# Two first weight loads as plain float32, the input in two transfers, and the angles' sines later, in a fused two-block transformer kernel

## The chip, the cores and the metric

The kernel runs on one core of one Trainium2 chip. The metric is the device time of one execution in microseconds (us). Three runs of the kernel before gave 1520.52, 1523.52 and 1526.42 us, so the median is 1523.52 us. The profile is of one more execution, which took 1524.71 us; the span that its trace covers is 1522.6 us.

## The reference

A sequence of 256 positions with 1024 features passes through two transformer blocks. The change touches the opening of the first block and one side computation for the second. Cut to that:

```python
# first block
h = rms_norm(x, norm_mix_g)                 # x is 256 x 1024
proj = h @ w_in                             # 1024 x 7168: b, c, x, a, g, gate_sc, gate_cf
cf = (cf_a + bias_a) * sigmoid(cf_g + bias_g)
y_cf = causal_depthwise_conv(cf, cf_conv_w)         # 31 taps
y_sc = sc_b * causal_depthwise_conv(sc_c * sc_x, sc_conv_w)   # 3 taps
# ... output projections, memory attention, an expert layer with gathered rows
# second block: attention with rotary positions, sines and cosines of
# positions * frequency, and with a bias by distance, then an MLP
```

Everything is float32.

## The kernel before

Features lie on the 128 partitions, the 256 positions along the free axis, so a projection of two output tiles (256 output features) is: two PSUM banks, each summed over eight 128x128 weight pieces `k`. One weight load is 1 MB (128 x 2048 words) and holds the pieces of two such tiles. The loads are numbered in the order of the list `LOADS`: 0 is for tiles g0 and g1, 1 for a0 and a1, 2 for g2 and g3, 3 for a2 and a3, and so on up to 7 (a6, a7); then follow, block by block, `c`, `x`, `b`: load 8 is c0 and c1, load 9 is x0 and x1, load 10 is b0 and b1, load 11 is c2 and c3, load 12 is x2 and x3, load 13 is b2 and b3.

Precision is kept by splitting. ScalarE copies a load from `raw` into a rounded part `w_hi` (line 1086), then VectorE or GpSimd takes the rest, `w_lo = raw - w_hi` (line 508). Activations are split in the same way into `x_hi` (line 1063, ScalarE) and `x_lo` (line 1438, VectorE). TensorE makes three matmuls of each pair (lines 678 to 680: hi by hi, hi by lo, lo by hi). `raw`, `w_hi` and `w_lo` are rings of three slots each (`RING = 3`). `LO_BY` says by name which engine subtracts: GpSimd has load 2 and 5, and every load from 8 to 19; VectorE has 0, 1, 3, 4, 6 and 7.

Each engine has its own instruction stream, written out by hand, and the order within it is the order of the code; engines wait on semaphores.

- SyncE issues the transfers: `x`, the small vectors, loads 0 and 1, constants, the memory input, positions, subkeys, and then the loads from 2 on. Load `i` waits until the `w_lo` of load `i - 3` is made (its slot of `raw` is then free).
- ScalarE: `round_to(n)` makes `w_hi` up to load n; `drain(name, i)` calls `ahead(name, i)` first (`round_to` up to two loads beyond this tile's load) and then copies the tile out of PSUM. The rounding of load `i` also waits until the last tile of load `i - 3` is finished, since it overwrites its halves. ScalarE squares `x` for the norm, makes load 0's `w_hi`, takes the square root (line 1105), splits the normed tiles, drains g0 to g7, then waits for `rope_arg` (line 1179), takes two `Sin` activations (lines 1180 and 1181), and only then goes on with c0.
- VectorE: waits for the vectors, makes load 0's `w_lo`, takes the reciprocal (line 1419), and alternates norm tiles (line 1454) with `x_lo` tiles. In the loop over the a tiles it drains each one (line 1512), and between a6 and a7 it runs `rope_angles` (lines 1484 to 1504), a chain in which every instruction waits for the one before it (`link`) and which reads and writes SBUF alone. Then come convolution taps (line 1540, sums in PSUM) between the drains of x and b tiles.
- TensorE: the sums of squares (line 728), then the tiles in the order of the list. There are four accumulation banks; a tile waits until the tile four before it has been drained. Thus x1 waits for a7's drain, and x2 for b0's.

The change and the steps of the prediction touch `linear_wide` (line 695), `linear` (682), the ScalarE stream from line 1161 to 1190, the VectorE stream from 1477 to 1522, `load` (526) and `wait_halves_free` (497).

Of the kernel before, what the change touches and what calls it, by code (L numbers as in the profile page):

```python
# [24 lines left out]
P = 128  # L25
SEQ = 256
# [141 lines left out]
for _, _, _e in TILES:  # L168
# [6 lines left out]
            )  # L175
BY_DVE = range(LOAD_OF["pq", 12], LOAD_OF["up", 6])
WHOLE = range(BEFORE_GATHERS + 1, LOAD_OF["gb", 7] + 1)
SLOTS = 11
# [16 lines left out]
for _i in range(len(LOADS)):  # L195
    HI_COUNT.append(_i + 1 - sum(_j <= _i for _j in WHOLE))
    RAW_COUNT.append(sum(_j % RING == _i % RING and _j not in WHOLE for _j in range(_i + 1)))
    if _i in WHOLE:
        LO_BY.append(None)
        continue  # L200
    _e = "pool" if _i % 3 == 2 and _i not in BY_DVE or LOADS[_i] in DVE_BUSY else "dve"
    _seen[_e] += 1
    LO_BY.append((_e, _seen[_e]))
# [46 lines left out]
def two_blocks(nc, T):  # L250
    ctx = ExitStack()
    with ctx:
# [165 lines left out]
        subkeys_landed = sem("subkeys_landed")  # L418
        x_landed = sem("x_landed")
        mem_landed = sem("mem_landed")  # L420
# [76 lines left out]
        def wait_halves_free(eng, i):  # L497

            if i >= RING and i - RING not in WHOLE:
                eng.wait_ge(acc_ready, LAST_TILE[i - RING] + 1)  # L500
            elif i - RING in WHOLE:
                eng.wait_ge(acc_ready, max(LAST_TILE[OCCUPANT[at]] for at in slots_of(i)[1:]) + 1)
# [19 lines left out]
        def _(sp):  # L522
            sp.dma_start(x_res[:].rearrange("p (t s) -> p t s", t=DT),
                         T["x_t"].rearrange("(t p) s -> p t s", p=P)).then_inc(x_landed, 16)

            def load(i):
                name, b = LOADS[i]
                if i >= RING and i - RING not in WHOLE:
                    engine, n = LO_BY[i - RING]
                    sp.wait_ge(w_lo_ready[engine], n)  # L530
                elif i - RING in WHOLE:
                    sp.wait_ge(acc_ready, LAST_TILE[OCCUPANT[i % RING]] + 1)
                sp.dma_start(ring(raw, i), T[name][b]).then_inc(raw_landed[i % RING], 16)
# [35 lines left out]
        def _(pool):  # L569
# [13 lines left out]
            def subtract_to(last):  # L583
                while n_lo[0] <= min(last, len(LOADS) - 1):
                    if n_lo[0] not in WHOLE and LO_BY[n_lo[0]][0] == "pool":
                        w_lo_split(pool, g, n_lo[0])
                    n_lo[0] += 1
# [44 lines left out]
        def _(pe):  # L632
# [24 lines left out]
            def linear_whole(name, which, wname, b, cols, lo=0, rows=P):  # L657

                w = whole_slot(wname, b)
                for j, i in enumerate(which):  # L660
                    out = open_tile(name, i)
                    for k in range(DT):
                        at = k * cols + lo + j * P
                        pe.wait_ge(h_ready, DT + k + 1)
                        mm = nc.tensor.matmul(by_chunk(out[0:rows, 0:SEQ]), w[:, at:at + rows], h_tile(k),  # L665
                                              start=(k == 0), stop=(k == DT - 1))
                    mm.then_inc(acc_ready, 1)

            def halves(x, k, cols=slice(0, SEQ)):
# [149 lines left out]
            for b in range(4):  # L819
                if b == 0:  # L820
                    linear_wide("g", range(2), "w_in", 16, "h1")
                else:
                    linear("g", range(2 * b, 2 * b + 2), "w_in", 16 + b, "h1", DT, 256)
                linear("a", range(2 * b, 2 * b + 2), "w_in", 12 + b, "h1", DT, 256)
                if b == 1:
# [217 lines left out]
        def _(act):  # L1043
# [34 lines left out]
            def round_to(last):  # L1078
                while n_hi[0] <= min(last, len(LOADS) - 1):
                    i = n_hi[0]  # L1080
                    n_hi[0] += 1
                    if i in WHOLE:
                        continue
# [76 lines left out]

            act.wait_ge(x_landed, 16)
            square("mix", lambda k: None, x_res)
            act.wait_ge(filled, 8)
            round_to(0)
            root("mix")
            split_all("h1", normed_tile("mix"), h_norm)
            round_to(1)
            for b in range(4):
# [8 lines left out]
                elif b == 2:  # L1177
                    split_all("mem", normed_tile("mem"), mem_raw)
            act.wait_ge(rope_arg, 2)
            s.activation(sin_t[NOPE:QHB, :], sin_t[NOPE:QHB, :], ACT.Sin).then_inc(rope_ready, 1)  # L1180
            s.activation(cos_t[NOPE:QHB, :], cos_t[NOPE:QHB, :], ACT.Sin).then_inc(rope_ready, 1)
            for b in range(4):
                for i in range(2 * b, 2 * b + 2):
                    drain("c", i, ct(c_buf, i))
                ahead("x", 2 * b)
                ahead("b", 2 * b)
            for i in range(8):
                drain("gsc", i, ct(gate_sc, i), ACT.Sigmoid)
# [221 lines left out]
        def _(dve):  # L1410
# [57 lines left out]
            def subtract_to(last):  # L1468
                while n_lo[0] <= min(last, len(LOADS) - 1):
                    if n_lo[0] not in WHOLE and LO_BY[n_lo[0]][0] == "dve":  # L1470
                        w_lo_split(dve, w_, n_lo[0])
# [4 lines left out]

            dve.wait_ge(vec_landed, 16)
            subtract_to(0)
            norm_split("mix", x_res, "norm_mix_g", h_norm, "h1")
            subtract_to(1)  # L1480

# [613 lines left out]
```

## Time and profile before

| | |
|---|---|
| median of three runs | 1523.52 us |
| the profiled execution | 1524.71 us |
| its span | 1522.6 us |
| TensorE (PE) busy | 1341.1 us, 88% |
| VectorE (DVE) busy | 957.4 us, 63% |
| ScalarE (ACT) busy | 523.3 us, 34% |
| GpSimd (POOL) busy | 559.6 us, 37% |

In the rows below, PE is TensorE, PEld its weight load, DVE is VectorE, ACT is ScalarE, POOL is GpSimd and SP is SyncE. Times are in us from the start of the span, "ns" apart. A row of the timeline is: start, duration, engine, line, operation, what it writes and reads with their shapes, the number of instructions merged, and in brackets how long the engine sat idle before it and what released it. A matmul's duration reaches to its modelled end; matmuls overlap, so the distance from one start to the next is the rate. PEclk is the share of full speed that TensorE's clock was granted (1.00 is 2.4 GHz, 0.50 is 1.2 GHz).

### The profile page before, as it was taken

To read this page: it belongs to the slowest core of one execution; us is meant where nothing else is said; L and a number is where in the kernel's file an instruction comes from. 1 tells how busy PE (TensorE), PEld (TensorE's weight loads), DVE (VectorE), ACT (ScalarE), POOL (GpSimd) and SP (SyncE) were. 2 spreads that over 40 slices of the span, in tenths; PEclk is the share of its full clock that TensorE was granted. 3 is DMA by queue.
4 is the path that set the end of the run, shared out by engine and by line. 5 is a ranking of instruction groups with operands and counts; after the bars stand their busy time and mean duration, and the time that the engine had idled before them with its cause. 6 is when DMAs were issued, how large, how long until landed. Compare 5 with 4: busy or idle time off the path is not lost.

```text
span 1522.6 us, 26124 instructions
## 1 busy us (share of the span) xinstructions
PE 1341.1 (88%) x10156; PEld 1280.4 (84%) x10156; DVE 957.4 (63%) x2043; ACT 523.3 (34%) x993; POOL 559.6 (37%) x348
## 2 busy tenths in 40 slices
PE   6999999899897868787878887978899999899996
PEld 6989999798897868786878877878785789899996
DVE  4698955765379585857676677755424447673563
ACT  6444454455443212121212221211226455444341
POOL 1377851321364546454535453545002000022230
PEclk9999999899999999898999998999999999999998
DMA  7445553352359999999999999999930134245450
GB/s 279 162 156 176 194 173 134 138 173 95 121 197 421 421 422 421 422 422 422 422 421 420 420 420 422 421 422 422 393 141 1 32 135 167 86 164 199 164 192 28
DMA packets 58071, 397.40 MB, mean 261 GB/s; under 512 B 6272, under 2 KB 9856, under 8 KB 10368
## 3 DMA queue, kind: packets, MB, share of 16 engines
q0 software_dynamic: 36864, 268.45, 42.5%
q1 hardware_dynamic: 21120, 127.76, 23.7%
q8 instruction: 58, 0.95, 0.3%
q14 instruction: 29, 0.24, 0.0%
HBM read 395.14 MB, written 1.05 MB: 260 GB/s over the span
## 4 chain that ended last, share of the span: by engine, by line
PE 49%; DMA 22%; DVE 15%; issue 8%; ACT 3%; POOL 2%; DVEq 0%; POOLq 0%; SPq 0%; ACTq 0%
DMA rows_late<-peer_uv_dram,stage 21%; PE bank L678 11%; PE bank L679 10%; PE bank L680 10%; PE bank L665 6%; PE bank L891 5%; DVE rows_late L1827 4%; PE bank L728 2%; ACT w_hi L1086 1%; POOL w_lo L508 1%; PE bank L789 1%; DMA rows_late<-peer_uv_dram,expert 1%; DVE w_lo L508 1%; POOL rows_late L608 1%; DVE probs L1775 1%
## 5 line engine op out<-in xcount | busy, mean ns | idle before, releaser
L508 POOL TENSOR_TENSOR w_lo<-raw,w_hi 128x2048 fp32r<-128x2048 f32 x49 | 227.5, 4645 | 517.5 <-ACT w_hi L1086 517.5
L891 PE MATMUL bank<-h_norm,rows_late 128*128 128x128 f32 x2816 | 331.7, 281 | 31.5 <-ACT h_norm L1254 31.5
L891 PEld LDWEIGHTS bank<-h_norm,rows_late 128*128 128x128 f32 x2816 | 327.5, 197 | 34.8 <-ACT h_norm L1254 34.8
L1827 DVE SCALAR_TENSOR_TENSOR rows_late<-rows_late,squares 128x1024 f32<-128x1024 f32 x176 | 213.7, 1228 | 135.0 <-DMA rows_late<-peer_uv_dram,stage 130.8
L891 PE MATMUL bank<-h_norm,rows_early 128*128 128x128 f32 x1280 | 176.2, 305 | 92.2 <-ACT h_norm L1254 92.1
L891 PEld LDWEIGHTS bank<-h_norm,rows_early 128*128 128x128 f32 x1280 | 170.0, 218 | 98.9 <-ACT h_norm L1254 98.9
L608 POOL DMA_INDIRECT rows_late<-peer_uv_dram,stage x165 | 197.0, 1194 | 136.1 <-PE bank L891 79.9
L508 DVE TENSOR_TENSOR w_lo<-raw,w_hi 128x2048 fp32r<-128x2048 f32 x55 | 133.5, 2429 | 129.0 <-ACT w_hi L1086 123.0
L678 PE MATMUL bank<-x_hi_a,w_hi 128*128 128x256 f32 x704 | 204.6, 291 | 10.9 <-DVE x_lo_a L1438 6.0
L1086 ACT ACTIVATE w_hi<-raw 128x2048 fp32r<-128x2048 f32 x104 | 197.7, 1904 | 47.5 <-PE bank L680 47.0
L678 PE MATMUL bank<-x_hi_b,w_hi 128*128 128x256 f32 x640 | 189.0, 295 | 20.6 <-POOL w_lo L508 10.7
L679 PE MATMUL bank<-x_lo_a,w_hi 128*128 128x256 f32 x704 | 200.6, 285 | 0.0
L680 PE MATMUL bank<-x_hi_a,w_lo 128*128 128x256 f32 x704 | 200.5, 285 | 0.0
L679 PE MATMUL bank<-x_lo_b,w_hi 128*128 128x256 f32 x640 | 185.5, 290 | 0.0
L680 PE MATMUL bank<-x_hi_b,w_lo 128*128 128x256 f32 x640 | 185.2, 289 | 0.0
L1254 ACT ACTIVATE h_norm<-const,weight 128x128 f32<-128x128 f32 x256 | 82.0, 390 | 291.5 <-DVE weight L1821 279.1
L608 POOL DMA_INDIRECT rows_early<-peer_uv_dram,stage x75 | 89.6, 1195 | 169.2 <-PE bank L891 145.8
L678 PEld LDWEIGHTS bank<-x_hi_a,w_hi 128*128 128x128 f32 x704 | 136.4, 194 | 13.2 <-issue 6.4
L678 PEld LDWEIGHTS bank<-x_hi_b,w_hi 128*128 128x128 f32 x640 | 127.5, 199 | 23.0 <-POOL w_lo L508 11.5
L1827 DVE SCALAR_TENSOR_TENSOR rows_early<-rows_early,squares 128x1024 f32<-128x1024 f32 x80 | 97.1, 1225 | 65.7 <-DMA rows_early<-peer_uv_dram,stage 53.7
L679 PEld LDWEIGHTS bank<-x_lo_a,w_hi 128*128 128x128 f32 x704 | 136.5, 194 | 0.5
L680 PEld LDWEIGHTS bank<-x_hi_a,w_lo 128*128 128x128 f32 x704 | 136.5, 194 | 0.0
(297 smaller groups left out, 2007.5 us busy)
## 6 DMA issues: line engine op xcount, KB each, us to landing
raw<-w_in_dram SPq DMA_DIRECT2D x28, 1024.0 KB, 4.9
raw<-w_up_dram SPq DMA_DIRECT2D x16, 1024.0 KB, 4.9
raw<-w_down_dram SPq DMA_DIRECT2D x16, 1024.0 KB, 4.9
rows_late<-w_in_dram SPq DMA_DIRECT2D x10, 1024.0 KB, 13.6
raw<-w_kv_dram SPq DMA_DIRECT2D x8, 1024.0 KB, 4.9
raw<-w_peer_q_dram SPq DMA_DIRECT2D x8, 1024.0 KB, 4.8
raw<-sc_w_out_dram SPq DMA_DIRECT2D x4, 1024.0 KB, 4.8
raw<-cf_w_pw_dram SPq DMA_DIRECT2D x4, 1024.0 KB, 4.9
```

Source lines behind the costliest of these rows:

```text
L508: api.tensor_tensor(ring(w_lo, i), ring(raw, i), ring(w_hi, i).bitcast(F32), ALU.subtract).then_inc(w_lo_ready[LO_BY[i][0]], 1)
L608: g.indirect_dma_start(out=expert_rows(k), out_offset=None, in_=T["peer_uv"], in_offset=bass.IndirectOffsetOnAxis(ap=stage_at[:, k:k + 1], ...
L665: mm = nc.tensor.matmul(by_chunk(out[0:rows, 0:SEQ]), w[:, at:at + rows], h_tile(k), start=(k == 0), stop=(k == DT - 1))
L678: nc.tensor.matmul(out, s_hi, m_hi, start=first, stop=False)
L679: nc.tensor.matmul(out, s_hi, m_lo, start=False, stop=False)
L680: return nc.tensor.matmul(out, s_lo, m_hi, start=False, stop=last)
L728: mm = nc.tensor.matmul(STAT[:, 0:SEQ], ones[:], ct(src, k), start=(k == 0), stop=(k == kt - 1))
L789: mm = nc.tensor.matmul(SCORE[u % 2][:, SEEN_BY[c]], q[:, c * P:(c + 1) * P], k[:, 0:(c + 1) * P], start=True, stop=True)
L891: mm = nc.tensor.matmul(ct(Y_ACC[c][t // 4], t % 4, P), expert_rows(k)[:, D + t * P:D + (t + 1) * P], ct(diag, k % DIAGS, P), start=False, ...
L1086: s.activation(ring(w_hi, i), ring(raw, i), ACT.Copy).then_inc(w_hi_ready, 1)
L1254: s.activation(ct(diag, k % DIAGS, P), ident, ACT.Copy, scale=weight[:, side * TOPK + k:side * TOPK + k + 1]).then_inc(diag_ready, 1)
L1827: w_.scalar_tensor_tensor(out=row, in0=row, scalar=1.0, in1=h_tok[:, c * D:(c + 1) * D], op0=ALU.mult, op1=ALU.mult, accum_out=pre[:, side ...
```

## The change

Loads 0 and 1 are not split. TensorE multiplies them as plain float32 from `raw`, as soon as each normed tile is there, in a new function `linear_plain`; their slots of `raw` are free only when their last tile is finished, so loads 3 and 4 wait for that. ScalarE's two roundings and VectorE's two subtractions for them go. VectorE makes all eight norm tiles first and the `x_lo` tiles after them. The input `x` comes in two transfers of four feature tiles each, and the squares of the second half wait for the second. The two `Sin` activations stand after the drains of the c tiles and the roundings up to load 21, twelve loads later.

```diff
+PLAIN = range(2)
-    HI_COUNT.append(_i + 1 - sum(_j <= _i for _j in WHOLE))
+    HI_COUNT.append(_i + 1 - sum(_j <= _i for _j in (*PLAIN, *WHOLE)))
...
-            sp.dma_start(x_res[:].rearrange("p (t s) -> p t s", t=DT),
-                         T["x_t"].rearrange("(t p) s -> p t s", p=P)).then_inc(x_landed, 16)
+            for half in range(2):
+                tiles = slice(half * DT // 2, (half + 1) * DT // 2)
+                sp.dma_start(x_res[:].rearrange("p (t s) -> p t s", t=DT)[:, tiles],
+                             T["x_t"].rearrange("(t p) s -> p t s", p=P)[:, tiles]).then_inc(x_landed[half], 16)
...
-                if i >= RING and i - RING not in WHOLE:
+                if i - RING in PLAIN:
+                    sp.wait_ge(acc_ready, LAST_TILE[i - RING] + 1)
+                elif i >= RING and i - RING not in WHOLE:
...
+            def linear_plain(name, which, i):
+                pe.wait_ge(raw_landed[i % RING], 16 * RAW_COUNT[i])
+                outs = [open_tile(name, n) for n in which]
+                for k in range(DT):
+                    pe.wait_ge(normed, NORMED["mix"] - DT + k + 1)
+                    for j, out in enumerate(outs):
+                        at = k * 256 + j * P
+                        mm = nc.tensor.matmul(out[:, 0:SEQ], ring(raw, i)[:, at:at + P], ct(h_norm, k),
+                                              start=(k == 0), stop=(k == DT - 1))
+                        if k == DT - 1:
+                            mm.then_inc(acc_ready, 1)
...
                 if b == 0:
-                    linear_wide("g", range(2), "w_in", 16, "h1")
+                    linear_plain("g", range(2), LOAD_OF["g", 0])
+                    linear_plain("a", range(2), LOAD_OF["a", 0])
                 else:
                     linear("g", range(2 * b, 2 * b + 2), "w_in", 16 + b, "h1", DT, 256)
-                linear("a", range(2 * b, 2 * b + 2), "w_in", 12 + b, "h1", DT, 256)
+                    linear("a", range(2 * b, 2 * b + 2), "w_in", 12 + b, "h1", DT, 256)
...
-            act.wait_ge(x_landed, 16)
-            square("mix", lambda k: None, x_res)
+            square("mix", lambda k: act.wait_ge(x_landed[k // 4], 16), x_res)
             act.wait_ge(filled, 8)
-            round_to(0)
             root("mix")
             split_all("h1", normed_tile("mix"), h_norm)
-            round_to(1)
...
-            act.wait_ge(rope_arg, 2)
-            s.activation(sin_t[NOPE:QHB, :], sin_t[NOPE:QHB, :], ACT.Sin).then_inc(rope_ready, 1)
-            s.activation(cos_t[NOPE:QHB, :], cos_t[NOPE:QHB, :], ACT.Sin).then_inc(rope_ready, 1)
             for b in range(4):
                 for i in range(2 * b, 2 * b + 2):
                     drain("c", i, ct(c_buf, i))
                 ahead("x", 2 * b)
                 ahead("b", 2 * b)
+            act.wait_ge(rope_arg, 2)
+            s.activation(sin_t[NOPE:QHB, :], sin_t[NOPE:QHB, :], ACT.Sin).then_inc(rope_ready, 1)
+            s.activation(cos_t[NOPE:QHB, :], cos_t[NOPE:QHB, :], ACT.Sin).then_inc(rope_ready, 1)
...
-            subtract_to(0)
-            norm_split("mix", x_res, "norm_mix_g", h_norm, "h1")
-            subtract_to(1)
+            norm("mix", x_res, "norm_mix_g", h_norm)
+            split_all("h1", h_norm)
```

## Rows read from the trace of the kernel before

**Rows 1.** The page's part 4: the chain that ended last, by engine.
```profile
PE 49%; DMA 22%; DVE 15%; issue 8%; ACT 3%; POOL 2%; DVEq 0%; POOLq 0%; SPq 0%; ACTq 0%
```

**Rows 2.** Stretch: start:end, length, PE busy (instructions), PEclk, DMA share, GB/s.
```profile
90.00:240.00 150.00, 150.00 (x1240) 1.00 0.55 190
```

**Rows 3.** The opening, timelines of ACT, DVE and PE.
```profile
6.48 2.56 ACT L1055 ACTIVATE squares<-x_res 128x256 f32<-128x256 f32 x8 [4.47 <-DMA x_res<-x_t_dram]
12.78 0.47 ACT L1105 ACTIVATE root_buf<-bank,eps 128x256 f32<-128x256 f32 x1
...
11.57 2.29 DVE L508 TENSOR_TENSOR w_lo<-raw,w_hi 128x2048 fp32r<-128x2048 f32 x1 [11.57 <-ACT w_hi L1086]
13.78 1.75 DVE L1419 RECIPROCAL rstd<-root_buf 128x256 f32<-128x256 f32 x1
...
7.04 5.71 PE L728 MATMUL bank<-squares,mean_d 128*128 128x256 f32 x16 [7.04 <-ACT squares L1055]
17.10 0.36 PE L678 MATMUL bank<-x_hi_a,w_hi 128*128 128x256 f32 x1 [4.36 <-DVE x_lo_a L1438]
25.65 0.39 PE L678 MATMUL bank<-x_hi_a,w_hi 128*128 128x256 f32 x1 [1.06 <-DVE w_lo L508]
```

**Rows 4.** A stretch of the first transfers: all engines, PEclk, DMA share, GB/s.
```profile
4.50:5.00 0.50, 0.00 (x0) 0.00 (x0) 0.00 (x0) 0.00 (x0) 0.00 (x0) 1.00 1.07 383
```

**Rows 5.** First and last of tile x1's 24 matmuls, from PE's timeline.
```profile
78.37 0.39 PE L678 MATMUL bank<-x_hi_a,w_hi 128*128 128x256 f32 x1
...
81.23 0.28 PE L680 MATMUL bank<-x_hi_a,w_lo 128*128 128x256 f32 x1
```

**Rows 6.** From the chain in order of time: eight plain float32 matmuls.
```profile
43.19 3.45 PE bank L728 x16
```

**Rows 7.** Around the angles and b0: timelines of ACT, DVE, POOL and PE.
```profile
78.57 1.92 ACT L1086 ACTIVATE w_hi<-raw 128x2048 fp32r<-128x2048 f32 x1
...
66.83 0.48 DVE L1512 SCALAR_TENSOR_TENSOR cf_in<-bank,vec,sig 128x256 f32<-128x256 f32 x1 [5.48 <-PE bank L680]
67.23 3.85 DVE L1484 CAST pos_row<-probs 128x256 f32<-128x256 int32 x1
...
71.91 0.29 DVE L1491 TENSOR_TENSOR dist<-dist,turns 128x128 f32<-128x128 f32 x1
...
73.41 0.34 DVE L1493 TENSOR_SCALAR sin_t<-pos_row,const 32x256 f32<-32x256 f32 x1
...
77.83 0.48 DVE L1512 SCALAR_TENSOR_TENSOR cf_in<-bank,vec,sig 128x256 f32<-128x256 f32 x1
...
93.48 0.42 DVE L1570 TENSOR_TENSOR c_buf<-bank,c_buf 128x256 f32<-128x256 f32 x1
...
66.31 4.62 POOL L508 TENSOR_TENSOR w_lo<-raw,w_hi 128x2048 fp32r<-128x2048 f32 x1 [0.46 <-ACT w_hi L1086]
80.57 13.69 POOL L508 TENSOR_TENSOR w_lo<-raw,w_hi 128x2048 fp32r<-128x2048 f32 x3 [9.64 <-ACT w_hi L1086]
...
85.19 0.39 PE L678 MATMUL bank<-x_hi_a,w_hi 128*128 128x256 f32 x1 [3.68 <-POOL w_lo L508]
```

**Rows 8.** Other meetings of DVE and POOL, from their timelines.
```profile
58.59 2.76 DVE L1438 TENSOR_TENSOR x_lo_b<-cf_acc,x_hi_b 128x256 fp32r<-128x256 f32 x8
60.25 5.59 POOL L508 TENSOR_TENSOR w_lo<-raw,w_hi 128x2048 fp32r<-128x2048 f32 x1 [15.82 <-ACT w_hi L1086]
...
428.67 4.61 POOL L508 TENSOR_TENSOR w_lo<-raw,w_hi 128x2048 fp32r<-128x2048 f32 x1 [0.71 <-ACT w_hi L1086]
...
432.69 0.62 DVE L1771 TENSOR_SCALAR part_i<-fin_i 128x32 uint32<-128x32 uint32 x1
```

**Rows 9.** PE's clock behind a pause; stretches as in Rows 2.
```profile
18.00:19.00 1.00, 1.00 (x7) 0.50 1.00 418
89.00:90.00 1.00, 1.00 (x8) 0.68 0.26 107
287.00:289.00 2.00, 2.00 (x17) 0.85 0.59 246
```

More of the change, by code:

```diff
@@ L195 @@
 for _i in range(len(LOADS)):
-    HI_COUNT.append(_i + 1 - sum(_j <= _i for _j in WHOLE))
+    HI_COUNT.append(_i + 1 - sum(_j <= _i for _j in (*PLAIN, *WHOLE)))
     RAW_COUNT.append(sum(_j % RING == _i % RING and _j not in WHOLE for _j in range(_i + 1)))
-    if _i in WHOLE:
+    if _i in WHOLE or _i in PLAIN:
         LO_BY.append(None)
@@ L418, in two_blocks @@
         subkeys_landed = sem("subkeys_landed")
-        x_landed = sem("x_landed")
+        x_landed = [sem(f"x_landed{i}") for i in range(2)]
         mem_landed = sem("mem_landed")
@@ L497, in wait_halves_free @@
         def wait_halves_free(eng, i):
-            if i >= RING and i - RING not in WHOLE:
+            if i >= RING and i - RING not in WHOLE and i - RING not in PLAIN:
                 eng.wait_ge(acc_ready, LAST_TILE[i - RING] + 1)
@@ L522, in _ @@
         def _(sp):
-            sp.dma_start(x_res[:].rearrange("p (t s) -> p t s", t=DT),
-                         T["x_t"].rearrange("(t p) s -> p t s", p=P)).then_inc(x_landed, 16)
+            for half in range(2):
+                tiles = slice(half * DT // 2, (half + 1) * DT // 2)
+                sp.dma_start(x_res[:].rearrange("p (t s) -> p t s", t=DT)[:, tiles],
+                             T["x_t"].rearrange("(t p) s -> p t s", p=P)[:, tiles]).then_inc(x_landed[half], 16)
             def load(i):
                 name, b = LOADS[i]
-                if i >= RING and i - RING not in WHOLE:
+                if i - RING in PLAIN:
+                    sp.wait_ge(acc_ready, LAST_TILE[i - RING] + 1)
+                elif i >= RING and i - RING not in WHOLE:
                     engine, n = LO_BY[i - RING]
@@ L584, in subtract_to @@
                 while n_lo[0] <= min(last, len(LOADS) - 1):
-                    if n_lo[0] not in WHOLE and LO_BY[n_lo[0]][0] == "pool":
+                    if n_lo[0] not in WHOLE and n_lo[0] not in PLAIN and LO_BY[n_lo[0]][0] == "pool":
                         w_lo_split(pool, g, n_lo[0])
@@ L1081, in round_to @@
                     n_hi[0] += 1
-                    if i in WHOLE:
+                    if i in WHOLE or i in PLAIN:
                         continue
@@ L1469, in subtract_to @@
                 while n_lo[0] <= min(last, len(LOADS) - 1):
-                    if n_lo[0] not in WHOLE and LO_BY[n_lo[0]][0] == "dve":
+                    if n_lo[0] not in WHOLE and n_lo[0] not in PLAIN and LO_BY[n_lo[0]][0] == "dve":
                         w_lo_split(dve, w_, n_lo[0])
```

## The prediction

> **What bounds the kernel now.** I read the page's chain first. It gives PE 49% and DMA 22% [rows 1]. The DMA part belongs to the expert rows, far behind the change, so all that the change can do is to let everything behind the opening start earlier or later. I then read the timelines of PE for its pauses in the first 240 us. There are few: before 7.04, before 17.10, before 25.65 and before 85.19 [rows 3, 7]; from 90 to 240 it is busy for all of 150.00 us [rows 2]. So PE is the bound of this stage, VectorE has pauses in it, and a shift of PE at 90 us should arrive at the end whole. The change works on all four pauses. What is to be seen: the first is a DMA wait, the second is the norm's chain, the third is the split of load 1, and the last is b0 waiting for GpSimd's `w_lo` of load 10, which is late because ScalarE rounded it only at 78.57, after the two sines [rows 7].
>
> **The opening.** Before, x1's 24 matmuls start 0.12 us apart (78.37 to 81.23), so a piece of a tile costs 0.36 us and a tile 2.88 [rows 5]. A plain float32 matmul of the same width is two instructions, eight of them take 3.45 us, 0.43 each [rows 6]. The 32 pieces of g0, g1, a0, a1 thus cost 32 x 0.43 = 13.8 us of PE instead of 32 x 0.36 = 11.5: the edit adds 2.3 us of matmul. What it takes away is the chain ahead of it.
>
> Input in halves: ScalarE squares from 6.48 [rows 3]. Half of x is 0.52 MB, and at 383 GB/s [rows 4] that is 1.37 us, so the first half should land at about 5.1 and the second as before. ScalarE's eight squares take 2.56 us, but PE takes 5.71 for their sums [rows 3], against 3.45 for the same work later [rows 6]: it works at about half speed at first, so PE, not ScalarE, ends this step (7.04 + 5.71 = 12.75, the root follows at 12.78). Starting at 5.7 instead of 7.04 they end at 11.4, if the full clock comes as soon after the start; if it comes at the same moment as before, the lost lead is worth up to half of 1.3, so 12.1. I take 11.6. The extra issue on SyncE is hidden: nothing waits for its queue before the loads, and they are bound by bytes.
>
> From root to product: root to reciprocal was 12.78 to 13.78, because VectorE subtracted load 0 until 11.57 + 2.29 = 13.86; without it the reciprocal can start half a microsecond behind the root. Root 11.6, reciprocal at 12.15 for 1.75, first norm tile at 13.9, ready at 14.4. PE starts at 14.45 (before 17.10, since x_hi and x_lo stood between). PE's pace (0.86 for the two pieces of one k) is slower than VectorE's, so nothing starves it. After a similar pause PE ran at clock 0.50 at 18 to 19 us, and around 89 it was still coming back [rows 9]; behind the pause before 85.19 this lasted 3.4 us, a loss of 1.7 us. I charge 1.7 here too: a1 ends at 14.45 + 13.8 + 1.7 = 29.95. Before it ended at 25.65 + 16 x 0.36 = 31.4 (rounded up by the slower first matmul: 31.45). Gain 1.5 us. Bounds: a gain of 3.2 if the shorter pause (2.8 us instead of 4.4) leaves the clock up, a loss of 0.3 if the sums end at 12.1 and the half clock lasts as long as behind the pause before 281.6, where PE still stood at 0.85 at 287 to 289 [rows 9], some 6 us, which costs 3.0.
>
> Is the next load there? Load 2 was issued behind the other inputs and its transfer is bound by bytes, so about 20 as before; ScalarE has time to round it at once (22), GpSimd subtracts for 4.6: 27, against 29.95. Cover 3 us; without it the gain would shrink by what it lacks. Load 3 now waits for g1, 14.45 + 6.9 + 1.7 = 23, instead of 13.9. I let it take 5 us to land, as a free queue needs (median on the page), 1.9 to round (as the 1.92 of [rows 7]) and 2.3 to subtract [rows 3]: 32.3, wanted by a2 at 29.95 + 5.76 = 35.7. Load 4 waits for a1, 30, is ready at 39.2, and is wanted at 30 + 11.5 + 3.45 (the memory's sums) = 45. Behind the waiting load 4 stands load 5, wanted six us later still. These new waits are hidden, by 3.4 us at the least. The x_lo tiles, moved behind the norm tiles, are done by 20 and wanted at 30.
>
> **The sines.** All times here are those of the old trace, the shift above apart. Before: PE finishes x1 at 81.25, waits until 85.19 and then works at 0.50 for 3.4 us; b0 effectively starts at 85.19 + 1.7 = 86.9. With the sines gone, ScalarE rounds load 10 as soon as load 7's halves are free: a6 ended at 66.8 (VectorE was waiting for it [rows 7]), a7 at 69.7, so the rounding is done at 71.65 and GpSimd asks for its subtraction at 71.7 instead of 80.57. That is the purpose, and taken alone b0 would lack nothing. The sines themselves cost nothing where they now stand: ScalarE waited there for PE every few us.
>
> But from 67.23 to 77.80 VectorE runs the angles, SBUF to SBUF, and in the old trace GpSimd is idle for all of it but the first four us. That first part shows the price: the CAST at 67.23 took 3.85 us and ended at 71.08, when GpSimd's subtraction (66.31 + 4.62 = 70.93) had ended [rows 7]. The TENSOR_SCALAR at 432.69 ended at 433.31, as GpSimd's from 428.67 ended at 433.28, where its neighbours need 0.2. The other way round, GpSimd's at 60.25 took 5.59, 1 us over its usual, while eight VectorE subtractions ran until 61.35 [rows 8]. So these two exclude each other for a whole instruction, and whoever is first holds the other up. Nothing in the old trace shows GpSimd asking in the middle of a chain whose instructions wait for each other; the gaps in it are some 0.04 us. Bounds: GpSimd gets in at no gap (delay 0) or at the first (4.5 us each time, 5.59 - 1.1). I take the first gap, since the eight subtractions that kept it out were issued back to back without waits, which the angles are not.
>
> The Trainium skill has a rule on just this (SBUF — State Buffer, "Who interferes with whom"): VectorE's copies, casts and tensor-scalar operations in two-port modes, and its operations with two SBUF inputs, contend with GpSimd for one shared pair, and "whoever issues first gets the shared pair for the whole instruction". By that rule each instruction of the chain is a new contest, and the sum is the forecast's; read as if a chain kept the pair, it would be the first rival's. The trace agrees on the exclusion (3.85 us for the cast) and is silent on the gap.
>
> Step by step. GpSimd takes load 10 at 71.87, behind the instruction in flight, until 76.4. The instruction that stood at 71.91 ends at 76.7: delay 4.5. ScalarE drains c0 and c1 (ended 69.7 + 5.76 = 75.5), rounds load 11 until 77.75, and GpSimd asks again. By then the chain, 4.5 late, is just before the instruction of 73.41. GpSimd holds until 82.35, and the rest of the chain, 77.80 - 73.41 = 4.4 us, ends at 86.8 instead of 77.80: delay 9.0. A third request can't come: load 12's rounding waits for x1. x1 waits for a7's bank, which VectorE drains behind the chain (before: drain 77.83 to 78.31, x1 at 78.37, already the last to come). So x1 starts at 87.35, after a pause of 9 us, at half clock for 3.4 to 6 us: loss 1.7 to 3.0, I take 2.2. b0 at 87.35 + 2.88 + 2.2 = 92.4 against 86.9: 5.5 us later. Load 10 is long there. x2 comes 11.5 later, 103.9, and needs b0's drain, which follows the chain by 93.9 - 77.8 = 16.1, so 102.9: no further wait. VectorE's own lag of 9 is made up in its pauses before 120 us.
>
> **Sum.** -1.5 + 5.5 = +4.0 us. On the profiled execution: span 1522.6 to 1526.6, time 1524.71 to 1528.7. That execution lies 1.2 us above the median of the runs, so I forecast 1523.52 + 4.0 = 1527.5.
>
> **Rivals.** First, GpSimd gets in at no gap, and asks in vain until 77.8. Load 10 is ready at 82.4, x1 ends at 81.25, PE pauses 1.1 us and keeps its clock: b0 at 82.4, 4.5 us earlier than 86.9. More can't be had even with no contest, since x2 needs b0's drain at 93.9, and 82.4 + 11.5 is just that. With the opening: -6.0, 1517.5. For it: back-to-back VectorE work did keep GpSimd out [rows 8]. Against: those had no waits.
>
> Second, only one block: the second request misses the chain or comes at its end. x1 at 82.85, b0 at 87.9, +1.0; with the opening -0.5, 1523.0. For it: my second meeting rests on ScalarE's order; against: it lies 4 us inside the delayed chain.
>
> Third, slower by a clear amount: the plain products run at the low clock throughout, because the pauses before them keep it there. The place is g0 to a1, the price 13.8 us more less the 1.7 charged, 12.1, the point from which it decides is a clock that is not back by about 20 us. With the rest: 1539.6. For it: the sums already begin slowly; against: PE came back within 6 us everywhere that I looked [rows 9].
>
> **Numbers.** Forecast 0.57, first rival 0.24, second 0.13, third 0.03; 0.03 for none of these. The forecast's own range is 1523 to 1531 (opening -3.2 to +0.3, the rest +5.0 to +6.3, and some 2 us of the median itself). The range given, 1516 to 1531, takes in the first rival. What a measurement of this kernel can tell from no change is about 0.5%, 7.6 us. Slower by more: the third rival and the forecast's upper tail, 0.10. Faster by more: a third of the first rival, 0.08. The rest, 0.82, is within.
>
> **What would show it.** Sums of squares from 5.7; first plain matmul near 14.5; load 2's `w_lo` before a1's end. Around 73 to 90 us: VectorE instructions of the angles that last 4.5 us, two of them, while GpSimd subtracts; x1 starting some 9 us behind x0's end; no pause before b0. If the angles run undisturbed and GpSimd's record is long instead, the first rival holds. If a pause stands before a2 or g4, my cover for the later loads was wrong.

## The result and the profile after

The changed kernel took 1530.74 us (median of 5 runs, 1527.81 to 1532.11) beside 1522.93 us (median of 5) for the kernel before: a ratio of 1.0049, 95% interval 1.0035 to 1.0063. It is slower by some 7.5 us (7.8 by the medians); 1527.5 was forecast, within 1516 to 1531, so the measured median lies only 0.3 us inside the range. Its profiled execution took 1527.81 us, span 1526.0, so it was the quickest of the five.

First the page's chain by engine, which answers to [rows 1] and shows nothing of it, as it should: the shares are the same.

```profile
PE 49%; DMA 22%; DVE 15%; issue 8%; ACT 3%; POOL 2%; DVEq 0%; POOLq 0%; ACTq 0%
```

The opening, from the timelines of ACT, DVE and PE, to be held against [rows 3] (x64 are all the plain products; where a row below shows fewer of them, its view ended there):

```profile
4.92 2.77 ACT L1074 ACTIVATE squares<-x_res 128x256 f32<-128x256 f32 x8 [2.91 <-DMA x_res<-x_t_dram]
12.05 1.28 ACT L1124 ACT_TABLE_LOAD   x1 [4.36 <-PE bank L746]
13.34 0.47 ACT L1124 ACTIVATE root_buf<-bank,eps 128x256 f32<-128x256 f32 x1
...
13.92 1.75 DVE L1435 RECIPROCAL rstd<-root_buf 128x256 f32<-128x256 f32 x1 [13.92 <-ACT root_buf L1124]
...
5.48 6.48 PE L746 MATMUL bank<-squares,mean_d 128*128 128x256 f32 x16 [5.48 <-ACT squares L1074]
16.34 16.53 PE L682 MATMUL bank<-h_norm,raw 128*128 128x256 f32 x64 [4.38 <-DVE h_norm L1441]
32.52 0.47 PE L696 MATMUL bank<-x_hi_a,w_hi 128*128 128x256 f32 x1
```

The squares start 1.6 us earlier, and yet the reciprocal starts at 13.92 instead of 13.78. The new row is the table load of the square root at 12.05: it came behind the sums (which end at 5.48 + 6.48 = 11.96), where before it ran while the sums still did, which ended at 12.75:

```profile
11.48 1.28 ACT L1105 ACT_TABLE_LOAD   x1
```

The plain products begin at 16.34, not 17.10, and end at 32.5 where the split ones ended at 31.45.

The angles, from the timelines of DVE, POOL, ACT and PE, against [rows 7]:

```profile
68.02 0.48 DVE L1527 SCALAR_TENSOR_TENSOR cf_in<-bank,vec,sig 128x256 f32<-128x256 f32 x1 [5.48 <-PE bank L698]
68.42 3.85 DVE L1499 CAST pos_row<-probs 128x256 f32<-128x256 int32 x1
...
72.84 0.23 DVE L1505 TENSOR_SCALAR turns<-dist 128x128 f32<-128x128 f32 x1
73.10 4.62 DVE L1506 TENSOR_TENSOR dist<-dist,turns 128x128 f32<-128x128 f32 x1
77.76 0.35 DVE L1504 TENSOR_SCALAR dist<-pos_row,pos_col 128x256 f32<-128x256 f32 x1
...
78.47 0.43 DVE L1506 TENSOR_TENSOR dist<-dist,turns 128x256 f32<-128x256 f32 x1
78.94 4.64 DVE L1508 TENSOR_SCALAR sin_t<-pos_row,const 32x256 f32<-32x256 f32 x1
...
87.65 0.48 DVE L1527 SCALAR_TENSOR_TENSOR cf_in<-bank,vec,sig 128x256 f32<-128x256 f32 x1
...
72.96 4.62 POOL L509 TENSOR_TENSOR w_lo<-raw,w_hi 128x2048 fp32r<-128x2048 f32 x1 [0.83 <-ACT w_hi L1105]
78.93 4.50 POOL L509 TENSOR_TENSOR w_lo<-raw,w_hi 128x2048 fp32r<-128x2048 f32 x1 [1.35 <-ACT w_hi L1105]
...
88.19 0.58 PE L696 MATMUL bank<-x_hi_a,w_hi 128*128 128x256 f32 x1 [8.69 <-DVE cf_in L1527]
```

Two instructions that took 0.29 and 0.34 us in [rows 7] now take 4.62 and 4.64, each beside a subtraction of GpSimd's that began within 0.14 us ahead of it, while or just after the instruction before it ran. a7's drain comes 19.6 us behind a6's, before 11.0. The pause of 3.68 us before b0 has become one of 8.69 before x1, whose releaser is VectorE.

A measure for the rest: the end of PE's first wait for GpSimd behind 250 us, less the start of a6's drain, VectorE's instruction that takes tile a6 out of PSUM (66.83 before, 68.02 after). It takes out the opening. The two rows, before and after:

```profile
270.66 0.55 PE L678 MATMUL bank<-x_hi_b,w_hi 128*128 128x256 f32 x1 [4.04 <-POOL w_lo L508]
277.17 0.38 PE L696 MATMUL bank<-x_hi_b,w_hi 128*128 128x256 f32 x1 [4.04 <-POOL w_lo L509]
```

Before it was 203.8 us; after, 277.17 - 68.02 = 209.2. I call it the middle.

### The profile page after: what moved, and what is told of

It reads as the page before. It is cut to its first block, busy times and chain, and to the rows that moved or that the text cites. A ratio compares the mean times of both kernels' runs of the same rounds, so it can differ in the third digit from the quotient of the medians.

```text
span 1526.0 us, 26055 instructions
## 1 busy us (share of the span) xinstructions
PE 1341.4 (88%) x10124; PEld 1279.3 (84%) x10124; DVE 961.8 (63%) x2041; ACT 520.0 (34%) x991; POOL 561.2 (37%) x348
## 4 chain that ended last, share of the span: by engine, by line
PE 49%; DMA 22%; DVE 15%; issue 8%; ACT 3%; POOL 2%; DVEq 0%; POOLq 0%; ACTq 0%
DMA rows_late<-peer_uv_dram,stage 21%; PE bank L696 10%; PE bank L697 10%; PE bank L698 10%; PE bank L670 6%; PE bank L910 4%; DVE rows_late L1842 4%; PE bank L746 2%; ACT w_hi L1105 1%; PE bank L682 1%; POOL rows_late L613 1%; PE bank L807 1%; DMA rows_late<-peer_uv_dram,expert 1%; POOL rows_early L613 1%; DVE hid L2025 1%
## 5 line engine op out<-in xcount | busy, mean ns | idle before, releaser
L910 PE MATMUL bank<-h_norm,rows_late 128*128 128x128 f32 x2816 | 328.1, 279 | 25.7 <-ACT h_norm L1270 25.7
L910 PEld LDWEIGHTS bank<-h_norm,rows_late 128*128 128x128 f32 x2816 | 324.1, 195 | 29.0 <-ACT h_norm L1270 29.0
L1105 ACT ACTIVATE w_hi<-raw 128x2048 fp32r<-128x2048 f32 x102 | 194.1, 1904 | 66.0 <-PE bank L698 58.5
L509 DVE TENSOR_TENSOR w_lo<-raw,w_hi 128x2048 fp32r<-128x2048 f32 x53 | 128.1, 2419 | 126.7 <-ACT w_hi L1105 122.5
L696 PE MATMUL bank<-x_hi_a,w_hi 128*128 128x256 f32 x672 | 195.1, 290 | 11.8 <-DVE cf_in L1527 8.7
L697 PE MATMUL bank<-x_lo_a,w_hi 128*128 128x256 f32 x672 | 191.0, 284 | 0.0
L698 PE MATMUL bank<-x_hi_a,w_lo 128*128 128x256 f32 x672 | 191.0, 284 | 0.0
L696 PEld LDWEIGHTS bank<-x_hi_a,w_hi 128*128 128x128 f32 x672 | 129.9, 193 | 13.3 <-DVE cf_in L1527 8.9
L697 PEld LDWEIGHTS bank<-x_lo_a,w_hi 128*128 128x128 f32 x672 | 130.0, 193 | 0.5
L698 PEld LDWEIGHTS bank<-x_hi_a,w_lo 128*128 128x128 f32 x672 | 129.8, 193 | 0.0
```

The lines of the kernel that those rows point to most:

```text
L509: api.tensor_tensor(ring(w_lo, i), ring(raw, i), ring(w_hi, i).bitcast(F32), ALU.subtract).then_inc(w_lo_ready[LO_BY[i][0]], 1)
L696: nc.tensor.matmul(out, s_hi, m_hi, start=first, stop=False)
L697: nc.tensor.matmul(out, s_hi, m_lo, start=False, stop=False)
L698: return nc.tensor.matmul(out, s_lo, m_hi, start=False, stop=last)
L910: mm = nc.tensor.matmul(ct(Y_ACC[c][t // 4], t % 4, P), expert_rows(k)[:, D + t * P:D + (t + 1) * P], ct(diag, k % DIAGS, P), start=False, ...
L1105: s.activation(ring(w_hi, i), ring(raw, i), ACT.Copy).then_inc(w_hi_ready, 1)
```

## Experiments

Each kernel is named by what it changes. Ratios are against runs of the kernel before on the same chip. The middle is taken from each one's trace. "Theory of the port" in the expectations is the prediction's: a GpSimd subtraction and a VectorE instruction from SBUF to SBUF exclude each other for a whole instruction, and one that is waiting gets in between two chained ones.

**Sines back.** The changed kernel with the three sine lines in their old place.

```diff
+            act.wait_ge(rope_arg, 2)
+            s.activation(sin_t ... ACT.Sin).then_inc(rope_ready, 1)
+            s.activation(cos_t ... ACT.Sin).then_inc(rope_ready, 1)
             for b in range(4):
...
-            act.wait_ge(rope_arg, 2)
```

> The changed kernel with the two sines back before the c tiles; plain loads and the input in halves stay. Theory of the port (GpSimd's subtractions of loads 10 and 11 now fall into VectorE's angles and hold them up twice, which costs 5.3 us net at b0): the angles run undisturbed, no instruction of them but the first cast over 1 us, PE pauses before b0 as in the old kernel, about 4 us, and all is about 1.2 us later than in the old kernel (a6's drain 68.0 instead of 66.8): median +0.5 to +2.5 us over before. Rival (the opening itself, with its loads held longer, makes the changed kernel slow and the sines are harmless): as slow as the changed kernel, +6 to +9 us.

1523.49 us against 1523.17, ratio 1.0000 (0.9986 to 1.0014). PE's timeline:

```profile
15.88 4.61 PE L682 MATMUL bank<-h_norm,raw 128*128 128x256 f32 x10 [4.38 <-DVE h_norm L1441]
85.73 0.58 PE L696 MATMUL bank<-x_hi_a,w_hi 128*128 128x256 f32 x1 [3.66 <-POOL w_lo L509]
```

The pause before b0 is back, the middle is 271.08 - 67.41 = 203.7 us. The time is a little under the +0.5 to +2.5 us that I expected. So plain loads and halves together bring nothing that these intervals show, and without the sines' move the loss is gone. The rival that blamed the opening is out.

**Sines only.** The old kernel with the three lines moved as in the change.

> The old kernel with nothing changed but the place of the two sines. Theory of the port: two of the angles' instructions last about 4.6 us each, x1 starts near 87 instead of 78.4, no pause before b0, and the time is 4.5 to 7 us over before. Rival (the opening is at fault): b0's pause goes and nothing replaces it, 4 us under before.

1528.04 us against 1523.17, ratio 1.0033 (1.0020 to 1.0046). The two long instructions and x1's pause, from DVE's and PE's timelines:

```profile
71.93 4.63 DVE L1491 TENSOR_TENSOR dist<-dist,turns 128x128 f32<-128x128 f32 x1
77.77 4.63 DVE L1493 TENSOR_SCALAR sin_t<-pos_row,const 32x256 f32<-32x256 f32 x1
...
87.01 0.58 PE L678 MATMUL bank<-x_hi_a,w_hi 128*128 128x256 f32 x1 [8.68 <-DVE cf_in L1512]
```

The prediction had them at 71.91 and 73.41 + 4.5, and x1 at 87.35. Middle 275.12 - 66.86 = 208.3. By the ratios this kernel loses 5.0 us and the changed one 7.5; their intervals overlap, and the 2.5 us between them stay open. The 0.9 us between the two middles are about what PE's clock behind x1's pause makes. PE's stretches (start:end, length, busy, PEclk), first of the changed kernel, then of this one:

```profile
92.00:93.00 1.00, 1.00 (x6) 0.50 0.00 0
89.00:90.00 1.00, 1.00 (x7) 0.57 0.00 0
```

The low clock lasted from x1's start at 88.19 to about 93, some 4.9 us, in the one, and from 87.01 to 89.9, some 2.9 us, in the other: 2 us more at half rate, which costs 1.0.

**GpSimd waits.** The changed kernel, and in GpSimd's loop:

```diff
+                    if n_lo[0] == LOAD_OF["b", 0]:
+                        pool.wait_ge(rope_arg, 2)
```

> The changed kernel, but GpSimd waits for the end of the angles before it subtracts load 10. Theory of the port: the angles take as long as in the old kernel, x1 is not held up, load 10 is ready 4.6 us behind the angles, PE pauses about 1.2 us before b0 and keeps its clock; b0 4.5 us earlier than the old kernel's effective 86.9, less the 1.2 that the opening costs: 2.5 to 4 us under before, some 10 us under the changed kernel. Rival (VectorE's long instructions come from something else than GpSimd's use of the memory, such as ScalarE's or the transfers'): they stay, and the time with them or above.

1517.92 us against 1523.17, ratio 0.9961 (0.9947 to 0.9976). The first cast is still held up, by load 9's subtraction as ever; nothing else in the angles is.

```profile
68.52 3.86 DVE L1501 CAST pos_row<-probs 128x256 f32<-128x256 int32 x1
79.12 0.48 DVE L1529 SCALAR_TENSOR_TENSOR cf_in<-bank,vec,sig 128x256 f32<-128x256 f32 x1
...
79.17 18.36 POOL L509 TENSOR_TENSOR w_lo<-raw,w_hi 128x2048 fp32r<-128x2048 f32 x4 [6.94 <-DVE sin_t L1521]
...
83.82 0.39 PE L698 MATMUL bank<-x_hi_a,w_hi 128*128 128x256 f32 x1 [1.02 <-POOL w_lo L509]
```

Middle 267.81 - 68.12 = 199.7, 4.1 less than before, where the prediction's first rival had 4.5. By the ratio the kernel is 5.9 us under before, more than the 2.5 to 4 expected; the profiled execution was the slowest of its five (1523.48), and the stretches that the wait touches are read from it, not the whole. One added wait turns the loss of the sines' move into the gain it could have been. That is as near to a proof as this study has that GpSimd's subtractions inside the angles, not the sines themselves, are the cause.

**One meeting.** The same wait, but only before load 11, so that load 10 still meets the angles.

```diff
+                    if n_lo[0] == LOAD_OF["c", 2]:
+                        pool.wait_ge(rope_arg, 2)
```

> The changed kernel, but GpSimd waits for the end of the angles only before load 11, not before load 10: one meeting instead of two. Theory of the port: exactly one instruction of the angles lasts about 4.6 us, a7's drain follows a6's by 15.1 us (two meetings 19.6, none 11.0), x1 starts near 83.7 and its pause is 4.2 us instead of 8.7. Rival (the delay isn't per meeting): two long ones again, or another sum.

One execution, 1522.91 us. DVE's and PE's timelines:

```profile
71.62 4.63 DVE L1508 TENSOR_TENSOR dist<-dist,turns 128x128 f32<-128x128 f32 x1
81.88 0.48 DVE L1529 SCALAR_TENSOR_TENSOR cf_in<-bank,vec,sig 128x256 f32<-128x256 f32 x1
...
82.42 0.58 PE L698 MATMUL bank<-x_hi_a,w_hi 128*128 128x256 f32 x1 [4.39 <-DVE cf_in L1529]
```

a7's drain follows a6's by 81.88 - 66.55 = 15.3 us, pause 4.4, middle 205.3. With none, one and two meetings the drain comes 11.0, 15.3 and 19.6 us behind: 4.3 for each.

**Fill awaited early.** The changed kernel, and ScalarE waits for `filled` at the second square and not behind the eighth.

```diff
-            square("mix", lambda k: act.wait_ge(x_landed[k // 4], 16), x_res)
-            act.wait_ge(filled, 8)
+            def x_there(k):
+                if k == 1:
+                    act.wait_ge(filled, 8)
+                act.wait_ge(x_landed[k // 4], 16)
+            square("mix", x_there, x_res)
```

> The changed kernel, but ScalarE waits for the constants' fill at its second square and not behind the squares, so that the square root's table load no longer carries the wait for the sums. Theory (the removed rounding had hidden that table load; now its 1.28 us lie on the opening's chain): table load at about 7.8 us, root directly behind the sums, everything behind it 1.3 us earlier than in the changed kernel (x1 at 86.9 instead of 88.2). Rival (PE's clock sets the opening): the root comes earlier, but PE is at half clock until the same moment, and less than 0.7 us arrives at x1.

1526.60 us against 1523.17, ratio 1.0023 (1.0010 to 1.0036), against 1.0049 for the changed kernel; the two intervals just touch. ACT and PE:

```profile
7.61 1.28 ACT L1124 ACT_TABLE_LOAD   x1
10.93 0.47 ACT L1124 ACTIVATE root_buf<-bank,eps 128x256 f32<-128x256 f32 x1 [2.04 <-PE bank L746]
...
13.93 6.28 PE L682 MATMUL bank<-h_norm,raw 128*128 128x256 f32 x28 [3.04 <-DVE h_norm L1445]
83.30 0.58 PE L696 MATMUL bank<-x_hi_a,w_hi 128*128 128x256 f32 x1 [8.68 <-DVE cf_in L1531]
```

The table load lies ahead of the sums' end again. PE's pause shrank from 4.38 to 3.04 us, and this time its clock stayed up. PE's stretches there (start:end, length, busy, PEclk), of this kernel:

```profile
14.00:15.00 1.00, 1.00 (x5) 1.00 1.09 357
15.00:16.00 1.00, 1.00 (x7) 1.00 1.13 330
16.00:18.00 2.00, 2.00 (x11) 1.00 1.09 408
```

and of the changed kernel:

```profile
17.00:18.00 1.00, 1.00 (x4) 0.50 1.05 439
20.00:21.00 1.00, 1.00 (x4) 0.50 0.00 0
21.00:22.00 1.00, 1.00 (x5) 0.81 0.00 0
```

a6's drain came at 63.14, 4.9 us earlier than in the changed kernel: 1.3 for the table load, 1.1 for sums that ended at 10.89 instead of 11.96, and 2.5 for the clock behind the pause. The 1.1 is the clock's too: single matmuls of the sums start 0.43 us apart at first and 0.22 apart later, and here that changed at about 9, in the changed kernel at about 11. So 1.3 of the 4.9 us belong to the edit and 3.6 to this execution. I had expected 1.3; the table load is settled, but the gain in time is not, because the clock after a 3 us pause is not the same in every execution (the next kernels show it low).

**One transfer.** The changed kernel with x in one transfer.

```diff
-            for half in range(2):
...
+            sp.dma_start(x_res[:] ... ).then_inc(x_landed[0], 16)
```

> The changed kernel with x in one transfer again. If the halves bring what the start of the sums shows: sums from 7.05 instead of 5.48, end near 13.0, first plain product near 17.4 instead of 16.3, a6's drain 0.5 to 1.5 us later than 68.0. Rival (the full clock comes at a set moment, whatever the start): the sums end less than 0.4 us later and the rest is as in the changed kernel.

One execution, 1535.43 us; sums from 6.95 to 13.68, first plain product at 18.06, a6's drain at 69.88, 1.9 us later than in the changed kernel, each a little later than expected. Over all thirteen traces the sums end at 10.89 to 12.04 us in the eight with halves (mean 11.6) and at 12.75 to 13.68 in the five without (mean 13.2). So the halves do bring the sums' end some 1.6 us forward.

**Halves only.** The old kernel with x in two transfers.

> The old kernel with nothing changed but x in two transfers. Theory (the rounding of load 0, which lands at 9.5, and the table load behind it stand on ScalarE until 12.76, and VectorE's subtraction until 13.86, so the sums are not what the norm waits for): sums end near 11.5 but the reciprocal still starts near 13.8 and the first product near 17.1; no gain. Rival (the sums' end sets the opening): 1.0 to 1.5 us earlier at the first product.

One execution, 1524.24 us, and the first product later than before, which neither theory had. From ACT's and PE's timelines:

```profile
4.61 2.79 ACT L1057 ACTIVATE squares<-x_res 128x256 f32<-128x256 f32 x8 [2.60 <-DMA x_res<-x_t_dram]
10.91 1.91 ACT L1088 ACTIVATE w_hi<-raw 128x2048 fp32r<-128x2048 f32 x1 [3.52 <-DMA raw<-w_in_dram]
...
18.46 0.55 PE L680 MATMUL bank<-x_hi_a,w_hi 128*128 128x256 f32 x1 [6.69 <-DVE x_lo_a L1439]
```

Load 0 was rounded at 10.91 and not at about 9.55: its last part landed at 10.83, 1.4 us later than before (9.47). That is not what the halves do as a rule: in the seven other traces with halves load 0 had landed at 9.57 to 9.87, in the five without at 9.40 to 9.51. With load 0 as punctual as there, the steps of the kernel before would give a first product at 17.1 to 17.5 (an estimate), as the theory has it; so its "no gain" is likely, but this one execution doesn't show it. What it does show is that in the old kernel load 0 is on the norm's path, and that sums which end earlier (11.77 here) don't help when it is late. a6's drain was at 68.20, the middle 203.6.

**Angles early.** Fill awaited early, and the angles moved ahead of the loop over the a tiles, where VectorE had 8 us and more to wait.

```diff
             dve.wait_ge(filled, 6)
+            dve.wait_ge(const_landed, 16)
+            dve.wait_ge(pos_landed, 32)
+            rope_angles()
             for i in range(8):
...
-                elif i == 6:
-                    dve.wait_ge(const_landed, 16)
-                    dve.wait_ge(pos_landed, 32)
-                    rope_angles()
```

> The changed kernel with the constants' fill awaited early (as in the run before) and the angles moved from between a6 and a7 to VectorE's pause behind the opening's x_lo tiles, where it waits 8 to 11 us for load 3. Theory of the port: they meet GpSimd's subtraction of load 2 there, once, which costs nothing since VectorE has the time; a7 is drained at once, x1, b0 and x2 start without a pause, PE works without one from the first product to 240 us. a6's drain at 63.1, and the place where PE later waits for GpSimd, 270.66 in the old kernel, comes at 261 to 262.5: 8 to 9.5 us under before. Rival (the taps or the load ring take over as the bound between 90 and 240 us): PE gets a new pause there, and less than 5 us are left.

1512.98 us against 1524.10, ratio 0.9937 (0.9922 to 0.9952): 9.6 us under before by the ratio. PE has no pause from the first product to 260 us:

```profile
14.43 5.89 PE L682 MATMUL bank<-h_norm,raw 128*128 128x256 f32 x13 [3.04 <-DVE h_norm L1445]
264.68 0.55 PE L696 MATMUL bank<-x_hi_b,w_hi 128*128 128x256 f32 x1 [4.04 <-POOL w_lo L509]
```

The angles met GpSimd once there, and it cost nothing on the path:

```profile
21.93 4.78 DVE L1510 TENSOR_TENSOR dist<-dist,turns 128x256 f32<-128x256 f32 x1
31.42 2.29 DVE L509 TENSOR_TENSOR w_lo<-raw,w_hi 128x2048 fp32r<-128x2048 f32 x1 [0.29 <-ACT w_hi L1105]
```

Middle 264.68 - 66.59 = 198.1, 5.7 under before. The marker at 264.68 is 2 to 4 us behind my 261 to 262.5, mostly since PE's clock fell after the pause of 3.04 us here (0.50 at 17 to 19 us) and had not in the kernel above; the sums also ended 0.5 us later.

> The kernel with early fill wait and early angles again, on the chip of its neighbours: 8 to 11 us under before. Its opening depends on whether PE's clock falls in the pause of 3 us behind the sums (both have been seen): a6's drain at 63.1 if not, 66.6 if it does.

Again: 1516.48 us against 1523.72, ratio 0.9948 (0.9929 to 0.9967), a6's drain at 65.70, middle 198.1. By the ratio that is 7.9 us under before, just short of the 8 to 11 expected. It beats the old kernel and the changed one.

> The same kernel with x in one transfer. If the halves are worth what the two profiles with and without them differ by (1.9 us at a6's drain): 1 to 2.5 us slower than its neighbour. Rival (the later start is made good by the clock): no difference.

1516.02 us, ratio 0.9951 (0.9934 to 0.9968): no difference that these intervals show, though a6's drain (68.40) is 1.8 to 2.7 us behind the two before it. The intervals are some 2.6 us wide to each side, more than the 1.6 us at the sums' end, so whether the halves are worth anything in the time stays open.

**Old kernel, angles early.**

> The old kernel (split opening, x in one transfer, sines in their old place) with nothing changed but the angles, moved ahead of the loop over the a tiles. Theory of the port: VectorE begins them at 25.6, behind load 1's subtraction, and meets GpSimd's subtraction of load 2 (25.15 to 30.09) with the first cast; they end near 37, load 3 is split at 39.4 instead of 36.0, so PE pauses 2 us before a2; the pause of 3.7 us before b0 and its 1.7 us of low clock go. Sum -3 to -4 us under before. Then the plain opening is worth another 5 to 7 us beside it (the kernel of the next run is 10 under). Rival (the plain opening is worth nothing once the angles are out of the way): 8 us under before or more, like the next run.

1520.03 us against 1523.72, ratio 0.9974 (0.9960 to 0.9989). DVE and PE:

```profile
25.61 4.72 DVE L1484 CAST pos_row<-probs 128x256 f32<-128x256 int32 x1
37.07 2.29 DVE L508 TENSOR_TENSOR w_lo<-raw,w_hi 128x2048 fp32r<-128x2048 f32 x1
...
39.86 0.55 PE L678 MATMUL bank<-x_hi_a,w_hi 128*128 128x256 f32 x1 [2.33 <-DVE w_lo L508]
```

As expected, VectorE had not the time in the split opening, and PE paused 2.33 us before a2. a6's drain came at 70.89, 4.1 us later than before, and the middle is 268.99 - 70.89 = 198.1 us, as in the three traces with the sines moved. So once the angles are early, it makes no difference where the sines stand: the whole 5.7 us can be had without moving them.

The plain opening (with halves and the early fill wait; the sines' place differs too) leaves VectorE free and took 3.6 us less on the same chip (1516.48 against 1520.03), where I had said 5 to 7. Compared run by run, the nine executions average 3.9 us less than these twelve, with a 95% interval of some 2 us to each side, and the nine with one transfer 3.5 us less; in the traces PE's first wait for GpSimd ends 5.2 us earlier (263.79 against 268.99). So this opening does pay beside early angles, and how its worth divides between its parts is open.

## Why the prediction was right, and where it was off

**The sines: right, by its own steps.** GpSimd did get in at the first gap between chained instructions, twice. The steps read 71.87, 76.7, 82.35, 86.8, x1 at 87.35; the kernel with the sines alone shows 71.93 + 4.63 = 76.56, 77.77 + 4.63 = 82.40, drain at 86.47, x1 at 87.01. The net was forecast at +5.5; the middle grew by 5.3 (changed kernel) and 4.4 (sines alone). The first rival, a chain that keeps GpSimd out, is refuted; so are the second, a single meeting, and the third, a low clock throughout the plain products (full again at 21.4 us). The first rival's 4.5 us were nearly reached, 4.1, once GpSimd was made to wait. But "more can't be had even with no contest" was wrong: with the angles moved ahead the middle shrank by 5.7, since that limit came from b0's drain behind the angles, and they no longer stand before it. The Trainium skill's rule that the first to issue holds the shared pair for the whole instruction (SBUF — State Buffer, "Who interferes with whom") thus holds between instructions that wait for each other too: VectorE's records last 4.62 and 4.64 us here, as long as GpSimd's.

**The opening: wrong in sign.** Forecast -1.5 with bounds of -3.2 to +0.3, measured a6's drain +1.2 (68.02 against 66.83), outside the bounds, and 66.6 to 68.1 over the four profiles with this opening. Term by term: first half of x at 5.1 forecast, 4.92 measured. Sums' end 11.6 forecast, 11.96. "Root 11.6", directly behind the sums: this step failed, the root came at 13.34 (the half microsecond from there to the reciprocal, at 13.92, held). The square root needs its table loaded, 1.28 us, and I let that pass as hidden, as it was before. It was hidden before by the order of waits. The removed rounding of load 0 had carried the wait for `filled`, so the table load behind it waited for nothing. With the rounding gone, two waits came before the root, for `filled` and for the sums (`stat_ready`). In these programs an activation carries one wait, the one written first; the second becomes a wait instruction of its own ahead of it, and the table load stands between the two. So the root itself waited for `filled`, long there, and the table load stood behind the wait for the sums. ScalarE's order in the built programs, the waits as they stand in them (before, then after):

```
L1084 wait raw_landed0
L1086 ACTIVATE w_hi<-raw [waits filled]
L1105 ACT_TABLE_LOAD
L1105 ACTIVATE root_buf<-bank,eps [waits stat_ready]

L1116 wait stat_ready
L1124 ACT_TABLE_LOAD
L1124 ACTIVATE root_buf<-bank,eps [waits filled]
```

The kernel with the fill awaited early shows it from the other side. The last term is the low clock: PE worked under it for 5.0 us (16.3 to 21.4), which costs 2.5 us and not 1.7, inside the 3.0 that I gave as the bound; the products themselves took 0.1 less than the 13.8. Together 0.4 for the sums, 1.3 for the table, 0.15 for the first norm tile and 0.7 for the products at their clock are the 2.6 us by which a1 ended late (32.5 against 29.95).

**The loads that wait for PE: right.** PE shows no pause from 16.34 to 79.5 us, where x0 ends (88.19 - 8.69), so the later loads 3 and 4 are covered.

**The total: right in sign, short in size, and inside the range with some luck.** 4.0 us forecast, 7.5 measured. The range was wide below, for the first rival, and narrow above; its own terms (+0.3, +6.3 and 2 us of the median) reach 1532, not 1531, and the opening left its bounds. The term that was mis-sized is the opening: +1.2 in place of -1.5 are 2.7 of the missing 3.5. The 0.8 left can't be placed. The traces of the two kernels differ by 6.5 us at PE's first wait for GpSimd behind 250 us, by 5.6 where the expert stage starts (472.45 against 466.85) and by 3.4 at the end, and over all thirteen traces the stretch from there to the end took 1053.3 to 1059.4 us for the same code. One profiled execution can't tell what a change brings to a median within some 3 us; the stretch that it touches can be read to 0.1.

## What to carry to other kernels

When an engine stops being late, ask what it now overlaps: a subtraction that starts 9 us sooner can hold another engine's chain, and a short chain of small dependent instructions is the worst to meet a long one, since each gap is a chance to lose 4.6 us. Move the chain to where its engine has time, or make the long instruction wait. And when an instruction is removed, see which waits stood before it: they now stand before the next one, and a table load that was hidden may come to stand behind them.

## What the runs showed of the hardware

- A GpSimd subtraction of 4.6 us (both operands and result in SBUF) stops a VectorE tensor-tensor or tensor-scalar instruction from SBUF to SBUF for its whole length, and gets in between two chained ones although the gap is about 0.04 us (4.62 and 4.64 us for instructions of 0.29 and 0.34). Convolution taps with their sums in PSUM were never held up (5.57 us for 14 in every trace).
- With the same opening and the same pause of 3.04 us, TensorE's clock stayed at 2.4 GHz in one execution (14 to 18 us at 1.00) and was at 1.2 GHz in three others (in one of them, 17 to 19 us at 0.50). Pauses of 3.9 us and more in the opening went with 0.50 every time, at their end or within 1.1 us of it.
- In the sums of squares at the start the clock's column says 1.00, but eight matmul pairs took 5.54 to 6.73 us where 3.45 is their full rate. Their starts lie 0.43 us apart until 9 to 13 us, and 0.22 apart from then on. The trace's first record of the clock stands at that moment (9.1 us in the earliest, 13.1 in the latest of thirteen), so ahead of it the starts tell the rate, and the column doesn't.
- One 1 MB input transfer cut in two: the first half landed at 4.6 to 4.9 us and the second at 6.0 to 6.4, the whole one at 6.4 to 6.5. The 1 MB load behind it landed 0.1 to 0.5 us later than behind the whole one, and in one of eight executions 1.3 to 1.4 us later.
